# Router product in four column groups, folded by a second product; picks ahead of gates and counts; norm epsilon inside the square sum

## The reference, cut to what matters

```
def rmsnorm(x, g):                       # 5 times; the mixers norm their parts too
    return x * rsqrt(mean(x*x) + 1e-6) * g

def moe_swiglu(x, ...):                  # layer 1 only, x is (256, 1024) after its norm
    logits = x @ w_router + b_router     # (256, 8)
    top_v, top_i = top_k(logits, 2)
    gates = softmax(top_v)
    combine = one_hot(top_i) weighted by gates          # (256, 8)
    for e in range(8):                   # w_gate, w_up (1024, 3584), w_down (3584, 1024)
        out += combine[:, e] * swiglu(x, w_gate[e], w_up[e], w_down[e])
```

## Time and profile before

| | |
|---|---|
| median of 3 runs | 1433.57 us (1431.04 to 1435.57) |
| profiled execution | 1429.53 us, span 1427.5 us |
| busy share of the span | PE 93%, DVE 33%, ACT 20%, POOL 7% |
| mean granted TensorE clock | 0.988 of full speed |
| read from HBM | 421 MB, 296 GB/s over the span |
| chain that ended last | PE 74%, DMA 14%, DVE 8%, others 4% |

### The profile page before, as it was taken

One profiled execution on the slowest core, in us unless ns is written; L12 is line 12 of the kernel. 1 busy time (PEld: TensorE's weight loads), 2 busy tenths in 40 slices (PEclk: granted clock), 3 DMA queues, 4 the chain that ended last, 5 costly groups with the idle time before them and its releaser, 6 DMA issues.

```text
span 1427.5 us, 18655 instructions
## 1 busy us (share of the span) xinstructions
PE 1331.2 (93%) x7760; PEld 752.4 (53%) x7760; DVE 467.2 (33%) x1045; ACT 279.5 (20%) x519; POOL 98.8 (7%) x115
## 2 busy tenths in 40 slices
PE   6989899999899969999999999999999999987775
PEld 5846599999675545444544444453433344332322
DVE  7998865554688540031101010110110100100002
ACT  3542443442363100000011010110100101000001
POOL 4530000000550000000000000000000000000000
PEclk9999999999999989999999999999999999999999
DMA  9533344548031197799999969989999999999994
GB/s 283 165 119 118 118 177 177 182 141 296 16 125 60 52 373 255 296 418 409 410 418 409 377 242 377 374 340 410 411 415 411 410 414 412 411 415 411 411 415 193
DMA packets 126734, 423.50 MB, mean 297 GB/s; under 512 B 21632, under 2 KB 23864, under 8 KB 118456
## 3 DMA queue, kind: packets, MB, share of 16 engines
q1 hardware_dynamic: 121464, 421.75, 75.6%
q10 hardware_dynamic: 5184, 0.52, 0.4%
HBM read 421.20 MB, written 1.05 MB: 296 GB/s over the span
## 4 chain that ended last, share of the span: by engine, by line
PE 74%; DMA 14%; DVE 8%; issue 1%; SPq 1%; ACT 1%; POOL 0%; DVEq 0%; ACTq 0%
PE psall L2318 14%; DMA m_ring<-in_moe_w_down_dram 12%; PE psall L2409 11%; PE psall L2332 8%; PE psall L2347 6%; PE psall L2032 4%; PE psall L2420 3%; PE psall L2249 3%; PE psall L2251 3%; PE psall L2130 3%; PE psall L2250 3%; PE psall L2295 2%; PE psall L2196 2%; PE psall L2382 2%; PE psall L2448 2%; PE psall L2231 1%
## 5 line engine op out<-in xcount | busy, mean ns | idle before, releaser
L2332 PE MATMUL psall<-m_ring,xeT 128*64 128x448 f32 x1024 | 204.2, 547 | 23.1 <-DMA m_ring<-in_moe_w_up_dram 23.1
L2409 PE MATMUL psall<-m_ring,hidT 128*64 128x512 f32 (+1 forms) x672 | 201.0, 597 | 15.6 <-DMA m_ring<-in_moe_w_down_dram 14.8
L2318 PE MATMUL psall<-m_ring,xeT 128*128 128x448 f32 x512 | 195.7, 543 | 0.8 <-DVE xeT L1897 0.8
L2332 PEld LDWEIGHTS psall<-m_ring,xeT 128*64 128x64 f32 x1024 | 73.8, 137 | 141.2 <-issue 140.0
L2318 PEld LDWEIGHTS psall<-m_ring,xeT 128*128 128x128 f32 x512 | 97.3, 191 | 94.1 <-issue 92.9
L2409 PEld LDWEIGHTS psall<-m_ring,hidT 128*64 128x64 f32 (+1 forms) x672 | 72.7, 154 | 134.9 <-issue 119.2
L1919 DVE TENSOR_TENSOR hid<-e_silu,psall 64x448 f32<-64x448 f32 x32 | 19.9, 623 | 354.9 <-ACT e_silu L1266 352.9
L1615 DVE TENSOR_TENSOR w_lo<-ring,w_hi 128x1024 fp32r<-128x1024 f32 x66 | 80.4, 1224 | 67.8 <-ACT w_hi L1210 67.6
L2347 PE MATMUL psall<-m_ring,xeT 128*32 128x448 f32 x1024 | 102.0, 542 | 0.0
L2249 PE MATMUL psall<-hnT_hi,w_hi 128*128 128x256 f32 x352 | 99.7, 283 | 0.7 <-DVE hnT_lo L1755 0.7
L2251 PE MATMUL psall<-hnT_hi,w_lo 128*128 128x256 f32 x352 | 99.5, 283 | 0.0
(11 more groups left out here) (327 smaller groups left out, 1455.8 us busy)
## 6 DMA issues: line engine op xcount, KB each, us to landing
m_ring<-in_moe_w_gate_dram SPq DMA_DIRECT2D x128, 896.0 KB, 20.1
m_ring<-in_moe_w_up_dram SPq DMA_DIRECT2D x128, 896.0 KB, 17.1
m_ring<-in_moe_w_down_dram SPq DMA_DIRECT2D x64, 1792.0 KB, 19.0
ring<-in_w_in_dram SPq DMA_DIRECT2D x10, 2048.0 KB, 13.1
ring<-in_ffn_w_gate_dram SPq DMA_DIRECT2D x5, 2048.0 KB, 10.6
ring<-in_ffn_w_up_dram SPq DMA_DIRECT2D x5, 2048.0 KB, 7.8
ring<-in_ffn_w_down_dram SPq DMA_DIRECT2D x5, 2048.0 KB, 8.0
ring<-in_w_out_dram SPq DMA_DIRECT2D x4, 2048.0 KB, 7.9
```

Source lines behind the costliest of these rows:

```text
L2318: ins = M(m_bank(key)[:, 0:MH], x[:, i, 0:P], weights(kind, i, s), start=(i == 0), stop=(i == KT - 1))
L2332: ins = M(m_bank(key)[64 * n:64 * n + 64, 0:MH], x[:, i, 0:64], weights(kind, i, s), start=(i == 0), stop=(i == KT - 1))
L2409: ins = M(y, hidT[:, r, 0:shape[0]], rows(r, 512 * n, 512), **ends)
```

## The change

Seven edits:

1. The router product runs in four column groups. Slice k goes to group k mod 4, with 32 stationary columns (8 of the router and 24 of zeros) into the PSUM partitions 32 (k mod 4) to +32; each group accumulates two slices. Each pair of slices waits only for its own `xT` bank. ACT copies all 128 partitions. The transposes L2269 become two products with a constant matrix `fold` (128 x 8, ones where the row's index mod 32 is the column) that transpose and add the four groups at once. `fold` is made on DVE.
2. The totals (two of the five count products) get a bank of their own, `("counts",)`, and are waited for later.
3. On DVE, constants and the clearing of `pickg` move ahead of the router's result. Gates, totals and `pickg` of item 0 move behind `take_tokens(0)`. `pick` and `pickg` have semaphores of their own (`v_pick`, `v_gate`).
4. `gate_up` waits for each piece of the gathered tokens where it is first used, not for the last piece ahead of everything.
5. Epsilon goes into the square sum as its starting value (1024 epsilon; 128 epsilon for the mLSTM heads); the missing factors sqrt(1024) and sqrt(128) go into `norm_scale`, into the output gate, and into the last norm's weights `gfin`, which are scaled once in the middle of the expert stage. L1348 and L1722 go.
6. The router's weights are loaded into the first 32 columns of `w_if`, after layer 1 has used them, and after all big weight chunks of the trunk.
7. PE's `picks` wait for `v_gate`.

The diff, cut to its core:

```diff
-            out.append((("logits",), "A", 5))
+            out.append((("logits",), "A", 7))
             out.append((("router",), "V", 4))
             out.append((("pos",), "V", 5))
+            out.append((("counts",), "V", 6))
...
-        w_rt = sb("w_rt", [P, KT, NE])
+        w_rt = w_if[:, :, 0:F_ROW]
...
-            nc.scalar.activation(logitsT[0:NE, :], bank(("logits",))[0:NE, 0:SEQ], ACT.Copy).then_inc(drained["A"], 1)
+            nc.scalar.activation(logits[:, :], bank(("logits",))[:, 0:SEQ], ACT.Copy).then_inc(drained["A"], 1)
...
             def norm_sum(t, scratch):
-                link(V.tensor_tensor_reduce(out=scratch, in0=x_res[:, t, :], in1=x_res[:, t, :], scale=1.0,
-                                            scalar=0.0, op0=ALU.mult, op1=ALU.add, accum_out=small[:, t:t + 1]))
-                V.tensor_scalar(small[:, t:t + 1], small[:, t:t + 1], 1.0 / DM, EPS, ALU.mult,
-                                ALU.add).then_inc(ms_ready, 1)
+                V.tensor_tensor_reduce(out=scratch, in0=x_res[:, t, :], in1=x_res[:, t, :], scale=1.0,
+                                       scalar=DM * EPS, op0=ALU.mult, op1=ALU.add,
+                                       accum_out=small[:, t:t + 1]).then_inc(ms_ready, 1)
...
-                    V.tensor_scalar(hn[:, t, :], x_res[:, t, :], small[:, t:t + 1], None,
+                    V.tensor_scalar(hn[:, t, :], x_res[:, t, :], small[:, t:t + 1], math.sqrt(DM), ALU.mult,
                                     ALU.mult).then_inc(hn_ready, 1)
...
+            V.tensor_reduce(out=fold[:, :], in_=ident[:, :].rearrange("p (q e) -> p e q", e=F_ROW)[:, 0:NE, :], axis=AX,
+                            op=ALU.add).then_inc(fold_ready, 1)
...
-            link(V.memset(pickg[:, :, :], 0.0))
-            choose(0, slice(0, 1))
+            choose_rows(0, slice(0, 1))
             take_tokens(0)
+            gates_of_tokens()
+            choose_gates(0, slice(0, 1))
             first_tiles()
...
+                if pos == 2 and p == 1:
+                    dve.wait_ge(s_gfin, 16)
+                    link(V.tensor_scalar(gfin[:, :], gfin[:, :], math.sqrt(DM), None, ALU.mult))
...
             for k in range(KT):
-                ins = M(bank(("logits",))[0:NE, 0:SEQ], w_rt[:, k, :], hnT[:, k, :], start=(k == 0),
-                        stop=(k == KT - 1))
+                q = 32 * (k % 4)
+                if k % 2 == 0:
+                    wait_drained(pe, ("xT", 1, 1, k // 2))
+                ins = M(bank(("logits",))[q:q + 32, 0:SEQ], w_rt[:, k, :], hnT[:, k, :], start=(k < 4), stop=(k >= 4))
             done(ins)
             open_bank(pe, ("router",))
+            pe.wait_ge(fold_ready, 1)
             wait_drained(pe, ("logits",))
             for t in range(NT):
-                ins = nc.tensor.transpose(bank(("router",))[:, t * NE:(t + 1) * NE],
-                                          logitsT[0:NE, t * P:(t + 1) * P], ident[0:NE, 0:NE])
+                ins = M(bank(("router",))[:, t * NE:(t + 1) * NE], logits[:, t * P:(t + 1) * P], fold[:, :],
+                        start=True, stop=True)
...
-                if c == 0:
-                    m_wait_drained(pe, ("xg", it, len(experts.k_pieces(it)) - 1), k)
+                def tokens_in(i):
+                    if c == 0:
+                        for j, (k0, k1) in enumerate(experts.k_pieces(it)):
+                            if i == k0:
+                                m_wait_drained(pe, ("xg", it, j), k)
```

More of the change, by code:

```diff
@@ L633, in trunk_kernel @@
         caps = moe("caps", [NI])
-        logitsT = moe("logitsT", [SEQ])
+        fold = moe("fold", [NE])
+        logits = moe("logits", [SEQ])
         n_list = sb("n_list", [P, 16], I32)
@@ L1776, in _ @@
             row = lambda ap: ap.unsqueeze(1).to_broadcast([P, NT, NE])
+            V.tensor_reduce(out=fold[:, :], in_=ident[:, :].rearrange("p (q e) -> p e q", e=F_ROW)[:, 0:NE, :], axis=AX,
+                            op=ALU.add).then_inc(fold_ready, 1)
             for e in range(NE):
-                ins = V.memset(desc[:, e:e + 1], float(NE - e))
+                V.memset(desc[:, e:e + 1], float(NE - e))
+            V.memset(want[:, :], 0.0)
+            for e in range(NI):
+                ins = V.memset(caps[:, e:e + 1], float(CAPS[e]))
             link(ins)
+            for rank, i in enumerate(ORDER):
+                V.memset(want[:, i - 1:i], float(rank))
+            link(V.memset(pickg[:, :, :], 0.0))
             dve.wait_ge(s_rt_in, 32)
@@ L1873, in second_tiles, with gates_of_tokens, choose_rows @@
                 dve.wait_ge(items_ready, 1)
-            def choose(it, col):
+            def gates_of_tokens():
+                dve.wait_ge(route_exp, 1)
+                link(V.tensor_scalar(R1(9), R1(8), 1.0, None, ALU.add))
+                link(V.reciprocal(R1(9), R1(9)))
+                link(V.tensor_tensor(R1(10), R1(9), R1(8), ALU.mult))
+                V.tensor_tensor(R(11), R(2), wide(9), ALU.mult)
+                link(V.tensor_tensor(R(12), R(5), wide(10), ALU.mult))
+                link(V.tensor_tensor(R(11), R(11), R(12), ALU.add))
+                V.tensor_copy(gateI[:, :, 0:1], R(11)[:, :, 0:1])
+                arrived(dve, ("counts",))
+                V.tensor_copy(O(0), bank(("counts",))[:, 0:NE]).then_inc(drained["V"], 1)
+                wait_drained(dve, ("counts",))
+            def choose_rows(it, col):
                 n = experts.tokens(it)
@@ L1879, in choose, with choose_gates @@
                 for t in range(NT):
-                    p = posI[:, t, col]
-                    g = gateI[:, t, col]
-                    V.tensor_scalar(pick[:, t, first:first + n], times[:, 0:n], p, None, ALU.is_equal)
+                    ins = V.tensor_scalar(pick[:, t, first:first + n], times[:, 0:n], posI[:, t, col], None, ALU.is_equal)
+                ins.then_inc(v_pick, 1)
+            def choose_gates(it, col):
+                for t in range(NT):
                     for lo, hi, tile, base in experts.slots(it):
                         a = P * tile + base
-                        ins = V.tensor_scalar(pickg[:, t, a:a + hi - lo], times[:, lo:hi], p, g, ALU.is_equal, ALU.mult)
-                ins.then_inc(v_pick, 1)
+                        ins = V.tensor_scalar(pickg[:, t, a:a + hi - lo], times[:, lo:hi], posI[:, t, col],
+                                              gateI[:, t, col], ALU.is_equal, ALU.mult)
+                ins.then_inc(v_gate, 1)
+            def choose(it, col):
+                choose_rows(it, col)
+                choose_gates(it, col)
             gcol = vec_col(1, "norm_ffn")
@@ L2276, in _ @@
             M(b[:, NE:2 * NE], ones[:, :], rt[:, 6, 0, :], start=True, stop=False)
-            M(b[:, NE:2 * NE], lower[:, :], rt[:, 6, 1, :], start=False, stop=True)
-            M(b[:, 2 * NE:3 * NE], ones[:, :], rt[:, 6, 0, :], start=True, stop=False)
-            done(M(b[:, 2 * NE:3 * NE], ones[:, :], rt[:, 6, 1, :], start=False, stop=True))
+            done(M(b[:, NE:2 * NE], lower[:, :], rt[:, 6, 1, :], start=False, stop=True))
+            open_bank(pe, ("counts",))
+            b = bank(("counts",))
+            M(b[:, 0:NE], ones[:, :], rt[:, 6, 0, :], start=True, stop=False)
+            done(M(b[:, 0:NE], ones[:, :], rt[:, 6, 1, :], start=False, stop=True))
             def event(ins):
@@ L2343, in quad @@
                     for i in range(UK * h, UK * h + UK):
+                        if shape[0] == 32:
+                            tokens_in(i)
                         for s in range(2):
@@ L2428, in picks @@
                 key = ("pt", p)
-                if k is None:
-                    pe.wait_ge(v_pick, 2 * p + 2)
+                pe.wait_ge(v_gate, 2 * p + 2 if k is None else later(NI + 1, 1, k))
                 m_open(pe, key, k)
```

49 lines of the change are left out of this document (19 added, 30 removed).

## The result

| us | before | changed |
|---|---|---|
| median (runs) | 1432.77 (5 runs, 1431.04 to 1435.57) | 1424.75 (5 runs, 1423.90 to 1426.47) |
| profiled execution, span, mean granted clock | 1429.53, 1427.5, 0.988 | 1424.28, 1422.3, 0.987 |

The ratio is 0.9949, 95% interval 0.9936 to 0.9961: 7.3 us less (5.6 to 9.2). The forecast was 6.13 us less, 1427.4, with a range of 1422.5 to 1431.5. A second set of five runs of the changed kernel, later in the study, gave 0.9960 (0.9946 to 0.9973), 5.7 us (6.5 by the medians). The two together say some 6.5 us (7.2 by the medians), so the first set alone is no evidence of a gain above the forecast.

The account below looks back on a forecast made before the run. PE was taken as the bound, with a chain from trunk to experts that hides nothing. 2.96 - 0.34 + 0.46 + 1.50 + 0.75 + 0.8 = 6.13 us off 1433.57 gave 1427.4 us, range 1422.5 to 1431.5.

Parts of the forecast that it names:

- the likeliest case: Between trunk and experts, the terms save 6.13 us in full: 1427.4 us, own range 1425 to 1430, chance 0.60.
- totals apart and picks first: Counts to gather: DVE skips waiting for two products, 0.46 us; fewer dependent small instructions at 0.20 us each save 1.50.
- wait per piece: Gather to first gate product: products follow the gather at once, 0.75 us saved; nothing to gain at other items.
- epsilon: At the norms: 0.1 us for each of four, 0.2 for L1722, some 0.2 for L1348; 0.8 in all, bounds 0.3 and 1.4.
- the estimate of 0.67 us from the last drain: Router product: four records remain behind the last drain, three steps of 0.097 us and one record of 0.38.
- comes only some 0.08 earlier: In the norms, the start of L1355's first half, which decides when POOL's power ends, shifts by only some 0.08 us.
- the plain count of 0.76: Norms: L1348's 0.15 us and a gap of 0.04, four times on the path; the shared port rule alone gives 0.3.
- The groups ran side by side: Rival at the router product: groups do not run side by side, 2.96 us goes, 1430.4; chance 0.12 together with the stream.
- POOL's power kept its 0.55 and 0.99 us: Rival at norms and heads: power of sums, inputs about a thousand times larger, takes longer; 1437.9 at 0.87 us more each; chance 0.04.
- the stream did not set the pace: Rival in the experts: time counts from the first load behind the ranks, only 3.4 us arrive, 1430.2; chance 0.12 with groups.
- the rival of 1425.5: At the gather: PE's idle stretch is shorter, the clock comes back in time and gives 1.9 us; chance 0.12.
- The rival in which the clock falls earlier: In the router: PE does less, so fold and counts at half clock cost about 0.6 us, the gather 1.8: 1429.8; chance 0.08.

Follow-up runs that it names:

- kept-busy profiles: Thrown-away products put into PE's idle times, on the kernel before (1427.02 us), changed (1418.23), column groups alone (1421.66) and wait per piece alone (1426.75).
- one set misplaced: Changed kernel with thrown-away products in five idle times, nine of them before layer 0's first S5 output product, where PE had work, instead of the second: 1417.27 us.

## Why the prediction was right

The steps of the likeliest case happened, in their place and order, and the time lay within the stated range; the median of 1424.75 us is just outside that case's own range (1425 to 1430). Term by term, with what the kept-busy profiles show:

| term | forecast | shown |
|---|---|---|
| column groups less folding product | 2.96 - 0.34 | 2.95 |
| totals apart and picks first | 0.46 + 1.50 | 2.02 |
| wait per piece | 0.75 | 0.95 |
| epsilon | 0.8 | about 1.35 |
| gather, more of it at half clock | 0 | a loss: 1.62 in this pair, 0.8 to 1.0 without the busy products |
| sum | 6.13 | 7.3 without the gather's loss, some 6.4 as the kernel is |

- *Router product.* The mechanism held, four side by side, and the estimate of 0.67 us from the last drain was 0.73. I counted the saving from 513.07, the first record's start, and left out that the product had waited 0.35 us behind ACT's drain (512.72); that wait went too.
- *Folding product, totals, picks.* 0.34 against 0.33 and 0.34; 1.96 against 2.02. The rule of 0.20 us for each dependent small instruction did this.
- *Wait per piece.* The first gate products even start 0.17 us before the gather's modelled end.
- *Epsilon*, the term most off. PE's idle time before layer 1's two norms' transposes fell from 5.39 to 5.03 and from 4.09 to 3.91. In layer 0 of the kept-busy pair it fell from 0.48 to 0.30 before the norm's transposes and from 0.72 to 0.31 at the end of the mixer. Behind the issue of the last load it is 0.23 less (45.03 to 44.80). Added up: about 1.35, above my 0.8, below the bound of 1.4. The kernel with the epsilon alone has the same 5.03 and 3.91, so these come from this part. The step that failed is "comes only some 0.08 earlier", and with it the 0.1 for each norm. In the norm before the router the first half's scaling (L1355) started 0.19 us after the sum was read (506.32, 506.51); now (L1359) it starts with it (508.59 both). POOL still ends 0.4 behind it, so the shift is 0.18 in place of 0.1. The four norms together gave 0.95, above the plain count of 0.76 and far above 0.3. In layer 1's first norm both halves' L1348 were on the chain, hence 0.36; at the heads it was 0.41 for the 0.2 charged, and why twice as much stays open.
- *Rivals.* The groups ran side by side; POOL's power kept its 0.55 and 0.99 us; the stream did not set the pace, since the shift of the gate product reached the last load in full and PE was busy throughout from 530 to 700 us. The clock came back no earlier, so the rival of 1425.5 fell, though the time came out at its place. The rival in which the clock falls earlier came true in part: fold and counts kept their time, but the gather got more of half clock. It took 6.49, 6.61 and 6.64 us in the three profiles with picks first and no busy products, 5.29 to 5.70 in the four with neither. I kept its time as it was; that should have been a cost of about 0.9. It nearly cancels the 1.2 us that the other terms gave in excess, so that the sum came out this close is partly luck.
- *What I missed* is that the clock moves everything outside the router as well, by more than the terms I was working out: 2 us in the trunk and 2 in the experts between two single profiles. The gain of 6.5 us over ten runs (7.2 by the medians) and the 6.4 us of the terms agree within the uncertainty. That 0.9949 came out and not 0.9960 needs no step of its own.

Open is why some kernels have runs at a mean clock of 0.99 (the wait per piece alone, the picks alone) and the kernel before in 50 runs never had one. Their code up to the router is the same.

The quickest version is the changed kernel kept busy: 1417.27 us with one set misplaced and 1418.23 with it put right, not distinguishable, some 14 us below the kernel before, of which half is the change and half the clock.

## What to carry to other kernels

Where two or three engines hand over to each other in turn, count the dependent instructions at their own price from the row next door, and look for the wait in front of a product as well as for its length. For differences under half a per cent, read each run's mean granted clock beside its time, and compare profiles stretch by stretch: a single part showed 4.6 us of which its own step made up 0.95. Where PE idles for some us ahead of work on the critical path, products that are thrown away can be worth as much as shortening the path: 6.9 us on the kernel before, against 6.5 for the change.

## What was not expected of the hardware

- Products of no use made the kernel quicker: the gather 3.84 us instead of 6.61, sixteen transposes 1.97 instead of 3.17 to 3.68, in all some 7 us. The Trainium skill (TensorE: Matmul & The Clock Gate, What's actually happening) says that activity releases the clock; here the release works with results that nobody reads. Not every stretch went: with the same products the gather of the last changed kernel still took 5.46 us, with 0.75 us of idle time ahead of it, as in the one that took 3.84.
- The start of the program varies between executions. The first product of layer 0 waits for its weights and began between 16.55 and 17.96 us in the profiles of this study. Its 64 records took 14.05 us to 17.10: with the clock at half from 18.2 to 21.6 us it was 15.77 (the wait per piece alone, kept busy). In the column groups' profile it was 17.03, with 6 records from 18 to 20 us where the kernel before has 11, though the view gives a clock of 1.00 there: for the first 20 us or so the clock column is no guide, and a run's mean clock does not count what happens there.
- Fp32 products in four column groups, 128 rows to 32 columns, 256 moving columns each: sixteen records of 0.38 to 0.40 us in 1.62 us, some 0.083 us from one to the next (the column groups alone, kept busy).
